# Two edits to a two-block transformer kernel: the last modulation group moved behind the first attention, and an expert gather with its operands exchanged

## The reference, cut to what matters

```python
# block 1
mod = silu(c) @ ada_w + ada_b                      # 1024 -> 6144
sh1, sc1, g1, sh2, sc2, g2 = split(mod, 6)
h = rms_norm(x, norm1_g) * (1 + sc1) + sh1
x = x + g1 * token_mixer(h, ...)                   # projections, state-space scan (SSM), attention
h = rms_norm(x, norm2_g) * (1 + sc2) + sh2
x = rms_norm(x + g2 * hier_moe(h, ...), final_g)   # 2 of 32 experts, 1024 -> 256 -> 1024
# token_mixer: attn = nsa_attention(...); ssm = s5_mixer(u, ...)
#   merged = sigmoid(gate_a) * (attn @ nsa_w_o) + sigmoid(gate_s) * (ssm @ ssm_w_o);  return merged @ w_out

# block 2 (its attention uses sh1, sc1, gt1)
sh1, sc1, gt1, sh2, sc2, gt2 = split(silu(c_2) @ w_mod + b_mod, 6)      # 1024 -> 6144
...
h2 = rmsnorm(x, g_pre_ffn) * (1 + sc2) + sh2
f = moe_ffn(h2, ...)                               # 4 of 32 experts
x = x + gt2 * rmsnorm(f, g_post_ffn)

# one expert of moe_ffn, for the tokens xe that chose it
gu = xe @ w_gu[e] + b_gu[e]                        # 1024 -> 2048
act = (clip(gu[:, 1024:], -7, 7) + 1) * swish(min(gu[:, :1024], 7))
y = act @ w_dn[e] + b_dn[e]                        # 1024 -> 1024, scattered back with its weight
```

## Time and profile before

| | |
|---|---|
| Median of 3 runs | 2037.44 us |
| The profiled execution's own time | 2032.57 us |
| Its span, first to last instruction | 2030.8 us |
| PE busy | 1836.9 us (90%) |
| DMA, mean over the span | 309 GB/s |
| DMA where the experts stream | 1.01 of its engines' time, about 417 GB/s |
| PEclk (granted clock, mean) | 0.977 |

### The profile page before, as it was taken

The page is one execution under the profiler, slowest core; times in us unless marked ns, Lnnn a source line. Parts: engine busy times, 40 slices in busy tenths (PEclk is TensorE's granted clock), DMA queues, the critical chain, the costliest instruction groups (busy, mean ns, idle before and its releaser), DMA issues.

```text
span 2030.8 us, 28209 instructions
## 1 busy us (share of the span) xinstructions
PE 1836.9 (90%) x10842; PEld 1001.1 (49%) x10857; DVE 529.3 (26%) x1213; ACT 390.5 (19%) x905; POOL 50.2 (2%) x109
## 2 busy tenths in 40 slices
PE   7999899987767899999989999988989999989987
PEld 4764677855534576677844333332333333333332
DVE  3676332131112132242432111111111111111112
ACT  4132453021101130343121100111110111100111
POOL 0040000000000010100010000000000000000000
PEclk9999899999878999999999999999999999999999
DMA  9969712418999662423455999999999899999997
GB/s 400 411 234 358 282 63 101 148 63 366 417 416 412 258 194 76 92 75 107 145 201 240 416 417 417 417 416 417 417 417 417 325 417 418 416 416 418 416 417 292
DMA packets 108634, 626.81 MB, mean 309 GB/s; under 512 B 11200, under 2 KB 15296, under 8 KB 50080
## 3 DMA queue, kind: packets, MB, share of 16 engines
q1 hardware_dynamic: 106688, 620.10, 75.7%
q0 software_dynamic: 1584, 4.33, 1.3%
q10 hardware_dynamic: 272, 1.05, 0.1%
HBM read 624.39 MB, written 1.05 MB: 308 GB/s over the span
## 4 chain that ended last, share of the span: by engine, by line
PE 58%; DMA 23%; SPq 10%; issue 4%; DVE 2%; ACT 2%; DVEq 0%; ACTq 0%
PE ps L465 56%; DMA ring<-in_w_gu_dram 15%; SPq L518 6%; DMA ring<-in_moe_w_gate_dram 4%; SPq L521 4%; PE ps L597 2%; DMA ring<-in_w_dn_dram 1%; DMA ring<-in_ada_w_dram 1%; DMA ring<-in_moe_w_down_dram 1%; DMA ring<-in_w_mod_dram 1%; ACT arena L1430 1%; SPq L491 0%; PE ps L593 0%; DVEq L1874 0%; PE ps L847 0%
## 5 line engine op out<-in xcount | busy, mean ns | idle before, releaser
L465 PE MATMUL ps<-ring,arena 128*64 128x512 f32 (+2 forms) x5376 | 888.2, 549 | 123.2 <-issue 55.1
L465 PEld LDWEIGHTS ps<-ring,arena 128*64 128x64 f32 (+1 forms) x5376 | 288.9, 129 | 664.1 <-issue 475.2
L465 PE MATMUL ps<-arena 64*128 64x512 f32 (+11 forms) x1492 | 258.1, 412 | 28.2 <-ACT arena L1430 15.5
L465 PE MATMUL ps<-hT,ring 128*128 128x256 f32 (+1 forms) x960 | 236.2, 401 | 1.6 <-DVE hT L1891 0.8
L465 PEld LDWEIGHTS ps<-hT,ring 128*128 128x128 f32 x960 | 179.7, 191 | 56.4 <-issue 33.0
L465 PEld LDWEIGHTS ps<-arena 64*128 64x128 f32 (+7 forms) x1494 | 126.8, 157 | 145.8 <-issue 93.1
L2246 DVE TENSOR_SCALAR arena<-ps 128x512 f32<-128x512 f32 (+1 forms) x34 | 23.0, 676 | 531.9 <-PE ps L465 531.9
L1430 ACT ACTIVATE arena<-ps 128x256 f32<-128x256 f32 (+5 forms) x191 | 104.3, 570 | 257.7 <-PE ps L597 131.9
L1696 ACT ACTIVATE arena<-ps,mod,gain 128x128 f32<-128x128 f32 x176 | 66.1, 458 | 426.3 <-PE ps L465 426.3
L1708 ACT ACTIVATE arena<-arena 128x512 f32<-128x512 f32 (+1 forms) x44 | 25.3, 574 | 590.3 <-DVE arena L2246 393.0
L465 PEld LDWEIGHTS ps<-arena,hN 128*128 128x128 f32 x960 | 110.7, 192 | 33.6 <-issue 17.8
(11 more groups left out here) (289 smaller groups left out, 911.1 us busy)
## 6 DMA issues: line engine op xcount, KB each, us to landing
ring<-in_w_gu_dram SPq DMA_DIRECT2D x256, 1024.0 KB, 20.3
ring<-in_w_dn_dram SPq DMA_DIRECT2D x128, 1024.0 KB, 23.1
ring<-dense_dram SPq DMA_DIRECT2D x56, 1024.0 KB, 12.5
ring<-in_moe_w_gate_dram SPq DMA_DIRECT2D x32, 1024.0 KB, 12.2
ring<-in_moe_w_up_dram SPq DMA_DIRECT2D x32, 1024.0 KB, 18.8
ring<-in_moe_w_down_dram SPq DMA_DIRECT2D x32, 1024.0 KB, 17.8
ring<-in_ada_w_dram SPq DMA_DIRECT2D x24, 1024.0 KB, 19.9
ring<-in_w_mod_dram SPq DMA_DIRECT2D x24, 1024.0 KB, 8.7
```

The source lines that it names most:

```text
L465: ins = nc.tensor.matmul(*a, start=start, stop=stop, **k)
```

## The change

Three things are done. (1) Group 5's eight tiles leave the stretch ahead of the attention. In the load order, four stand now behind `glu` and four ahead of `no` 2. TensorE multiplies four ahead of branch 0 and four ahead of branch 2, into bank 7 in place of 3, and transposes them into bank 6 between branch 3 and `w_out`. ScalarE's copies follow its two sigmoids. VectorE's sums with group 5 (L2027, L2073, L2074) follow the merge. (2) The tiles of group 4 are dealt out by 3, 3 and 2 in place of 4, 4 and 8. (3) In `further` of block 2, `gather` becomes `gather_strips`: the 32 one-hot columns are the stationary operand, and hN moves, a quarter of its 1024 columns in each of four strips of the array: 8 matmuls of 256 columns. The tokens then lie in rows; VectorE copies them to SBUF, TensorE transposes them (two transposes, `strips_turn`), and VectorE scales in two halves and shifts.

```diff
-        mod_chunks(24, 16)
+        mod_chunks(24, 8)
...
         for c in range(4):
+            if c % 2 == 0:
+                mod_chunks(32 + 2 * c, 4)
             chunk(("no", c), wcols("nsa_w_o", c * 256, c * 256 + 256), KD, 256)
...
-                if k == 0 and g >= 1:
+                if k == 0 and g == 5:
+                    pe.wait_ge(emptied, nth(emptied, ("gate", 7)))
+                elif k == 0 and g >= 1:
                     pe.wait_ge(emptied, nth(emptied, ("mod rows", g - 1)))
...
-            modulations(4)
+            modulations(3)
             ssm_step()
...
-            modulations(4)
+            modulations(3)
             ssm_step()
...
-            modulations(8)
-            turn_modulation(5)
+            modulations(2)
+            turn_modulation(4)
             while done_j[1] < 16:
                 ssm_step()
...
             pe.wait_ge(madeV, nth(madeV, "yD"))
-            pe.wait_ge(emptied, nth(emptied, ("mod columns", 5)))
+            pe.wait_ge(emptied, nth(emptied, ("mod columns", 4)))
             attention(1, units1)
...
                 b = 2 * ((c + 1) % 2)
+                if c % 2 == 0:
+                    modulations(4)
...
+            turn_modulation(5)
             pe.wait_ge(madeV, nth(madeV, ("mgd", 2)))
             for c in range(4):
                 w = weights(pe, ("wo", c))
+                if c == 2:
+                    pe.wait_ge(emptied, nth(emptied, ("mod columns", 5)))
...
-            def gather(s, xs_onehot):
-
-                for k in range(KD):
-                    for tt in range(TT):
-                        last = mm(ps[:, 3, k * MORE:(k + 1) * MORE], hN[:, tt, k * P:(k + 1) * P], xs_onehot[:, tt, :],
+            def gather_strips(s, onehot):
+
+                for tt in range(TT):
+                    for x in range(4):
+                        last = mm(ps[32 * x:32 * x + 32, 3, 0:256], onehot[:, tt, 0:MORE], hN[:, tt, x * 256:(x + 1) * 256],
                                   start=tt == 0, stop=tt == 1)
                 last.then_inc(s["gathered"], 1)
+
+            def strips_turn(s):
+
+                for h in range(2):
+                    last = transpose(ps[:, 3, 256 + h * P:256 + (h + 1) * P], glu[:, h * P:(h + 1) * P])
+                last.then_inc(s["rows_turned"], 1)
...
-                    gather(x, ohgM[:, :, 0:MORE])
+                    gather_strips(x, ohgM)
+                    pe.wait_ge(x["rows"], q + 1)
+                    strips_turn(x)
                     occupy(7, 4, True)
...
+            v.wait_ge(emptied, nth(emptied, ("mod columns", 5)))
+            step(tt_(mod2[:, 32:48, :], mod2[:, 32:48, :], B(cols[:, 1, 32:48], 2), ALU.add))
...
-                def xs_out(s, dst):
-                    src = ps[:, 3, 0:KD * MORE].rearrange("p (k s) -> p k s", s=MORE)
-                    step(tt_(dst, src, each(gs, MORE), ALU.mult))
+                def xs_out(s, dst, q):
+                    V.tensor_copy(glu[:, 0:256], ps[:, 3, 0:256]).then_inc(s["rows"], 1)
+                    v.wait_ge(s["rows_turned"], q)
+                    for h in range(2):
+                        src = ps[:, 3, 256 + h * P:256 + (h + 1) * P].rearrange("p (x s) -> p x s", s=MORE)
+                        tt_(dst[:, h::2, :], src, each(gs[:, h::2], MORE), ALU.mult)
+                    v.drain()
                     tt_(dst, dst, each(sh, MORE), ALU.add).then_inc(s["xs"], 1)
```

More of the change, by code:

```diff
@@ L440, in program @@
         STEPS = ("gather_onehot", "gathered", "xs", "spread_onehot", "spreadT", "spread", "hidden", "glu", "sig",
-                 "act", "turned", "actT", "down", "ys", "scattered")
+                 "act", "turned", "actT", "down", "ys", "scattered", "rows", "rows_turned")
         S = {(n, kind): {x: sem(f"moe{n}_{kind}_{x}") for x in STEPS} for n in (1, 2) for kind in ("first", "more")}
@@ L618, in modulation @@
                 w = weights(pe, ("mod", g, k))
-                if k == 0 and g >= 1:
+                if k == 0 and g == 5:
+                    pe.wait_ge(emptied, nth(emptied, ("gate", 7)))
+                elif k == 0 and g >= 1:
                     pe.wait_ge(emptied, nth(emptied, ("mod rows", g - 1)))
                 for m in range(4):
-                    last = mm(ps[32 * m:32 * m + 32, 3, :], cpad[:, k, :], w[:, m, :], start=k == 0, stop=k == KD - 1)
+                    last = mm(ps[32 * m:32 * m + 32, 7 if g == 5 else 3, :], cpad[:, k, :], w[:, m, :], start=k == 0, stop=k == KD - 1)
                 if k == KD - 1:
@@ L635, in turn_modulation @@
                 for b in range(4):
-                    last = transpose(ps[:, 2, b * P:(b + 1) * P], mod_row[:, b, :])
+                    last = transpose(ps[:, 6 if g == 5 else 2, b * P:(b + 1) * P], mod_row[:, b, :])
                 last.then_inc(filled, mark(filled, ("mod columns", g)))
@@ L644, in modulations @@
                     g, k = 1 + i // 8, i % 8
-                    if k == 2 and g >= 2:
+                    if k == 2 and 2 <= g <= 4:
                         turn_modulation(g - 1)
@@ L1466, in mod_rows @@
                 act_.wait_ge(filled, nth(filled, ("mod rows", g)))
-                copy(mod_row.rearrange("p a b -> p (a b)"), ps[:, 3, :]).then_inc(emptied, mark(emptied, ("mod rows", g)))
+                copy(mod_row.rearrange("p a b -> p (a b)"), ps[:, 7 if g == 5 else 3, :]).then_inc(emptied, mark(emptied, ("mod rows", g)))
             def mod_columns(g):
                 act_.wait_ge(filled, nth(filled, ("mod columns", g)))
-                src = ps[:, 2, :].rearrange("p (b m c) -> p m b c", m=4, c=32)
+                src = ps[:, 6 if g == 5 else 2, :].rearrange("p (b m c) -> p m b c", m=4, c=32)
                 if g < 3:
@@ L1735, in _ @@
             sigmoids("gates")
+            modulations(8)
+            mod_columns(5)
             moe_front(1)
@@ L2023, in attention @@
                         maxima(n, i + 2, units[i + 2])
-            v.wait_ge(emptied, nth(emptied, ("mod columns", 5)))
+            v.wait_ge(emptied, nth(emptied, ("mod columns", 4)))
             tt_(mod1[:, 16:48], mod1[:, 16:48], cols[:, 0, 16:48], ALU.add)
-            step(tt_(mod2[:, :, :], mod2[:, :, :], B(cols[:, 1, 0:48], 2), ALU.add))
+            step(tt_(mod2[:, 0:32, :], mod2[:, 0:32, :], B(cols[:, 1, 0:32], 2), ALU.add))
             V.memset(rtok[:, :], 1.0).then_inc(madeV, mark(madeV, ("shift", 1)))
@@ L2072, in _ @@
             tt_(gain[:, 4, :], mod2[:, 16:24, 0], cols[:, 1, 56:64], ALU.mult)
-            stt(gain[:, 5, :], mod2[:, 32:40, 0], 1.0, cols[:, 1, 64:72], ALU.add, ALU.mult)
-            tt_(gain[:, 0, :], mod2[:, 40:48, 0], cols[:, 1, 72:80], ALU.mult)
             v.drain()
@@ L2080, in _ @@
             clear_tables(1)
+            v.wait_ge(emptied, nth(emptied, ("mod columns", 5)))
+            step(tt_(mod2[:, 32:48, :], mod2[:, 32:48, :], B(cols[:, 1, 32:48], 2), ALU.add))
+            stt(gain[:, 5, :], mod2[:, 32:40, 0], 1.0, cols[:, 1, 64:72], ALU.add, ALU.mult)
+            tt_(gain[:, 0, :], mod2[:, 40:48, 0], cols[:, 1, 72:80], ALU.mult)
             for c in range(4):
```

10 lines of the change are left out of this document (5 added, 5 removed).

## The result

| | before | after |
|---|---|---|
| Median, 5 runs each | 2037.44 us (2036.07 to 2037.94) | 2026.39 us (2022.77 to 2029.75) |
| Ratio | | 0.9949 [0.9938, 0.9960] |
| The profiled execution's own time | 2032.57 | 2024.26 |
| Its span | 2030.8 | 2022.5 |
| PEclk, mean | 0.977 | 0.983 |

The changed kernel is faster by 11.0 us (8 to 12.6 by the interval). The two profiled executions differ by 8.3 us; the other 2.7 are that before's stood 4.9 us under its median and after's 2.1 under its own.

What follows compares the result with a forecast made beforehand. Group 5's arrival by DMA was taken to set the time ahead of the attention, TensorE behind it. Terms -12.5 + 7.7 - 0.8 = -5.6 us gave 2031.8 us from 2037.44, range 2027.3 to 2036.3.

Steps and rivals of the forecast that it cites:

- Ahead of the attention: Stretch before the first attention: without group 5 the attention starts at 198.3 instead of 210.86, gain 12.5 us.
- Behind it: Behind the attention, TensorE without a gap: eight tiles 7.1 and transposition 0.6 add 7.7 us, DMA causing no wait.
- The array's change of tiling: Around group 5's tiles behind the attention: each partition change under 0.1 us; by the skill's rule a few tenths in sum.
- Block 2's first further block: Gather to bias 1.6 us shorter, less 0.8 lost in `hidden_strips`: 0.8 us gained, ends 2.4 and -0.8.
- the lower clock from 1073 then falls on `hidden_strips`: Block 2's first further block: 1.7 us of `hidden_strips` at half rate instead of `occupy`, a loss of 0.8 us.
- The end of 2.4: Upper end of the gain in block 2's first further block, if the clock does not drop: 2.4 us.
- The second further block: Block 2's second such block: its gather is hidden by transfers, which TensorE waits for; gain 0.
- The scale: Forecast given on the scale of the runs' median, which stood 4.87 us above the profiled execution's 2032.57.
- the main case: Forecast with the clock mean near 0.58 behind the attention's start: 2029.5 to 2033.5 us, chance 0.58.
- neither well nor badly: Two rivals at the attention's start: clock full, 2028.8 us, chance 0.14; half clock longer, 2034.8 us, chance 0.12.
- The late SSM: Rival ahead of the attention: SSM ends at 200 instead of 195.5, gain 8.0, time 2036.3 us, chance 0.07.
- the late ring: Rival: moved tiles delay the first expert group, 2.5 us per tile past 13 us slack; slower by clock or ring 0.06.

Runs made afterwards that it cites:

- Experiment 2: Group 5 moved as in the change, old gather kept, against the kernel before: 2032.43 us, ratio 0.9979.
- experiment 5: Kernel before with seven one-matmul `occupy` between the old gather's eight pieces: 2035.47 us, ratio 0.9998 to before.
- experiments 3: New gather alone, group 5 left where it was, against the kernel before: 2029.43 us, ratio 0.9967.
- 8: Changed kernel with 18 unused 16-column products in TensorE's wait for the input at the program's start: 2043.59 us, ratio 1.0033 to before.
- experiment 10: Changed kernel with 64 unused 16-column products at the program's start: 2032.49 us, ratio 0.9976 to before.
- second run of 11: Changed kernel, but group 5 loaded in the old order and multiplied in TensorE's waits around the attention's start; repeat: 2017.94 us, ratio 0.9899 to before.

## Why the prediction was right, and where it was wrong

- **Ahead of the attention.** -12.5 foreseen, -12.36 measured. Each term is right to 0.1: SSM step 15 ended at 195.60 (195.5 foreseen), the last `ssm_out` at 196.71 (196.5), and TensorE waited 1.80 for the skip term (1.86). One row was misread without harm: 192.81 is not the end of group 4's tiles, which had ended at 189.6, but the start of group 5's behind `kc`; the same work in another order ended at 193.1.
- **Behind it.** +7.7 foreseen, +7.96 measured, on a TensorE without a gap; no DMA shows. Experiment 2 timed the two together at 4.3, foreseen 4.8.
- **The array's change of tiling.** Without group 5's rows, `glu` and the branches take 7.10 + 20.91 + 20.83 = 48.84 us by their starts; before they took 382.15 - 333.69 = 48.46. The 0.38 between them is all that four changes can have added there, so under 0.1 each. The Trainium skill says that a change of tiling mode drains TensorE ("TensorEngine Tiling (Array Packing)", Key Properties). The trace agrees with it in direction and with the prediction's few tenths in size, though nothing here separates a drain from other small delays.
- **Block 2's first further block: this step failed.** The term was -0.8. It had two parts. The gain ahead of the bias was right: 1.6 foreseen, 5.29 to 3.50 measured, 1.8. The other, "the lower clock from 1073 then falls on `hidden_strips`", +0.8, was wrong in kind: the earlier trace rows were read as a clock that falls at that time, whatever stands there. It fell because of the old gather, 32 records of 32 columns, each with a full 128x128 weight load, for 3.76 us. With the old gather it fell in three of three profiles here (and in two of three in the second block), with the new one it stayed at 1.00 in all nine profiles that have it, and experiment 5 kept it up by more work in the same old gather. So the block gives 2.7 where 0.8 was foreseen (4.35 against experiment 2's profile). The end of 2.4 that the text gave for "no drop of the clock" would have been the better value.
- **The second further block.** 0 foreseen, -0.99 measured: the down-projection waits in two pieces (2.62 and 0.49) and runs in 3.8 at the full clock, where the earlier trace rows have one wait of 3.51 and 5.32 at a lowered one. That is not the new gather's doing as far as shown. Over the nine profiles with it the block takes 28.8 in four, 29.5 in three, 29.8 and 30.3 in two (after has 28.82); with the old one 29.7 to 29.8 (29.4 in experiment 5), and 29.84 without any. The transfers do hide the gather, as the prediction said; what varies is the clock.
- **The scale.** The forecast took the median as standing 4.87 over the profiled execution after the change as well; it stood 2.13 over it. With executions 8 us and more apart, one profile places a median only to a few us; of the 5.4 us that the forecast is off, 2.7 are this.
- **The rivals.** The clock at the attention's start came as in the main case (0.60), neither well nor badly. The late SSM and the late ring did not come.
- **A term that the sum did not have.** The new gather also shortens TensorE's code by 14 records, and the idle time at block 2's first expert changes with the place of the code (experiments 3 and 8). In after this gave 0.3 us, in 3's profile 2.1.
- **Open.** Of the gather's timed 6.7 us (4.5 to 9.2) the 2.7 of the first block are shown. How much of the rest is the place of the code, and how much chance, is not: no run changed the gather with its number of records kept. The break at 34 is the same in before and after, so the move did not gain by it.

## What to carry to other kernels

A lowered clock belongs to the work that brought it, not to a time on the axis: when that work is exchanged, ask anew whether it falls at all, in more than one profile, since the same work brings it down in some and not in others. Where weights fill DMA and TensorE idles for "issue" inside a loop, look for the record at which its work breaks off, since a few records more or fewer anywhere ahead can move it and cost or give more than the edit itself; test an edit with its records balanced before its idea is given up. And work moved from a wait to a place without a gap is paid in full: look for other waits to put it in first (10 us here).

## What the runs showed of the hardware

- TensorE's list breaks off at places that depend on how many records stand ahead, in loops under full DMA: 18 products more at the program's start lengthened the idle time before a group's products from 11.5 to 16.0 us, and the kernel by 17 us; 128 records restored the old place. At block 2's first expert the idle time is 3.3 to 3.7 us in one piece or 0.4 and 1.5 to 1.9 in two, by the same count.
- 32 records of 32 moving columns under 128x128 weight loads, back to back (3.76 us), brought the granted clock from 1.00 to 0.50 in five of the six old gathers profiled, although TensorE was not idle in them; 16 records of 256 columns (1.07 us) did so in none of 18. 32 records of 48 columns (3.8 us, about 165 us into the program) did so in two of 14 profiles, those of experiment 10 and of the second run of 11.
